# The split weights start 44 instead of 48 bytes behind a multiple of 64, and the table of constants lies behind them

## What is computed

```python
for li in range(2):                                   # the first block
    x = x + 0.5 * swiglu(rmsnorm(x, g[0]), ffn_w_in[li, 0], ffn_w_out[li, 0])     # 1024 -> 2*2816 -> 1024
    x = x + (hgrn2_mixer if li == 0 else mla_mixer)(rmsnorm(x, g[1]), ...)
    x = x + 0.5 * swiglu(rmsnorm(x, g[2]), ffn_w_in[li, 1], ffn_w_out[li, 1])
    x = x + sigmoid(rmsnorm(x, g[3]) @ ple_w_gate[li]) * (p[li] @ ple_w_in[li])
x = rmsnorm(x, final_norm)
for layer in range(2):                                # the second block
    x = x + (even_mixer if layer == 0 else odd_mixer)(rms_norm(x, ...), ...)
    x = x + conv_ffn(rms_norm(x, ffn_norm[layer]), w_up, conv_w, conv_b, w_down)  # 1024 -> 2*2816 -> 1024
```

## The kernel before

| tile | offset modulo 64 | what uses it |
|---|---|---|
| raw, x, x_hi, x_lo, h_hi, h_lo, h_val, c_hi, c_lo, q_both, x_lo_2 | 0 | loads, activations |
| cst | 12 | first constant `mean1024` at 12, `freq` is one column, all others behind it at 16 |
| rstd, rstd_tok | 16 | norms |
| sumsq, ln_ms, ln_tok | 32 | norms |
| w_hi, w_lo, all slots and 128-column tiles | 48 | the split weights |
| tmp, zero, eps | 48 | squares, clearing |
| work, small, k_rope, cos, sin | 52 | everything inside the mixers and hidden layers |

## Time and profile before

### The profile page before, as it was taken

One profiled execution on the slowest core, in us unless ns is written; L12 is line 12 of the kernel. 1 busy time (PEld: TensorE's weight loads), 2 busy tenths in 40 slices (PEclk: granted clock), 3 DMA queues, 4 the chain that ended last, 5 costly groups with the idle time before them and its releaser, 6 DMA issues.

```text
span 1822.1 us, 36683 instructions
## 1 busy us (share of the span) xinstructions
PE 1750.2 (96%) x14492; PEld 1714.1 (94%) x14492; DVE 1190.6 (65%) x1764; ACT 957.6 (53%) x1097; POOL 351.6 (19%) x280
## 2 busy tenths in 40 slices
PE   7999899989999899999999999999899999989998
PEld 7999899979999899998998999988799999989998
DVE  6665688976565666556456555665477766567776
ACT  5444667764444754444345444565455455655553
POOL 2000500020004600036663000566400020020001
PEclk9999999999999999999999999999999999999999
DMA  5656323335555445544444555434245443345552
GB/s 218 225 190 242 128 101 115 99 119 208 198 190 185 156 176 193 188 141 135 137 138 154 187 187 185 170 128 151 93 170 199 177 180 139 117 162 185 185 206 92
DMA packets 45168, 298.25 MB, mean 164 GB/s; under 512 B 5024, under 2 KB 5408, under 8 KB 15920
## 3 DMA queue, kind: packets, MB, share of 16 engines
q1 hardware_dynamic: 45104, 297.38, 46.1%
HBM read 296.31 MB, written 1.05 MB: 163 GB/s over the span
## 4 chain that ended last, share of the span: by engine, by line
PE 80%; DVE 10%; ACT 5%; issue 3%; DMA 1%; POOL 0%; SPq 0%; ACTq 0%; DVEq 0%
PE wk L379 15%; PE wk L380 15%; PE wk L381 15%; PE acc L379 8%; PE acc L380 8%; PE acc L381 8%; DVE sumsq L678 2%; DVE x_lo L457 1%; PE wk L1033 1%; PE wk L391 1%; PE wk L390 1%; PE wk L389 1%; DVE x L422 1%; ACT w_hi L325 1%; ACT tmp L619 1%
## 5 line engine op out<-in xcount | busy, mean ns | idle before, releaser
L325 ACT ACTIVATE w_hi<-raw 128x2048 fp32r<-128x2048 f32 (+5 forms) x300 | 533.3, 1788 | 405.8 <-PE wk L381 333.8
L380 PE MATMUL wk<-x_lo,w_hi 128*128 128x256 f32 x2560 | 715.9, 280 | 0.0
L379 PE MATMUL wk<-x_hi,w_hi 128*128 128x256 f32 x2208 | 624.7, 283 | 19.0 <-DVE x_lo L457 13.3
L2603 POOL TENSOR_TENSOR w_lo<-raw,w_hi 128x512 fp32r<-128x512 f32 (+1 forms) x274 | 350.8, 1316 | 1455.7 <-ACT w_hi L325 1455.7
L381 PE MATMUL wk<-x_hi,w_lo 128*128 128x256 f32 x2208 | 618.0, 280 | 0.0
L351 DVE TENSOR_TENSOR w_lo<-raw,w_hi 128x2048 fp32r<-128x2048 f32 (+2 forms) x218 | 483.9, 2221 | 171.5 <-ACT w_hi L325 171.5
L380 PEld LDWEIGHTS wk<-x_lo,w_hi 128*128 128x128 f32 x2560 | 483.5, 189 | 0.4
L379 PEld LDWEIGHTS wk<-x_hi,w_hi 128*128 128x128 f32 x2208 | 421.4, 191 | 25.2 <-DVE x_lo L457 15.4
L381 PEld LDWEIGHTS wk<-x_hi,w_lo 128*128 128x128 f32 x2208 | 416.8, 189 | 0.0
L379 PE MATMUL acc<-h_hi,w_hi 128*128 128x256 f32 x1376 | 389.5, 283 | 16.3 <-DVE h_lo L2192 4.8
L381 PE MATMUL acc<-h_hi,w_lo 128*128 128x256 f32 x1376 | 385.9, 280 | 0.0
(11 more groups left out here) (323 smaller groups left out, 2138.4 us busy)
## 6 DMA issues: line engine op xcount, KB each, us to landing
raw<-w_ffn_loop SPq DMA_DIRECT2D x120, 1024.0 KB, 4.8
raw<-w_conv_loop SPq DMA_DIRECT2D x60, 1024.0 KB, 4.8
raw<-w_mla_loop SPq DMA_DIRECT2D x18, 768.0 KB, 4.3
raw<-w_hgrn_loop SPq DMA_DIRECT2D x10, 896.0 KB, 4.6
raw<-w_ple_gate SPq DMA_DIRECT2D x8, 1024.0 KB, 4.7
raw<-w_odd_loop SPq DMA_DIRECT2D x10, 768.0 KB, 4.2
raw<-w_even_loop SPq DMA_DIRECT2D x6, 1024.0 KB, 4.8
raw<-w_odd_proj SPq DMA_DIRECT2D x6, 1024.0 KB, 4.8
```

Of the source, the lines that this page charges most:

```text
L325: nc.scalar.activation(w_hi[slot][:, 0:n], raw[slot][:, 0:n], ACT.Copy).then_inc(S("hi_ready"), 1)
L379: nc.tensor.matmul(dst, hi, a_hi, start=start, stop=False, skip_group_check=True)
L380: nc.tensor.matmul(dst, hi, a_lo, start=False, stop=False, skip_group_check=True)
L2603: last = nc.gpsimd.tensor_tensor(w_lo[slot][:, a:b], raw[slot][:, a:b], w_hi[slot][:, a:b].bitcast(F32), ALU.subtract)
```

## The change

The line that allocates `cst` moves from behind `par` to behind `w_lo`. Nothing else is edited; every engine's list of instructions is the same, in the same order, with the same waits. What differs is addresses:

```diff
         par = sb("par", [P, N_PARAMS])
-        cst = sb("cst", [P, N_CONSTS])
         rstd = sb("rstd", [P, SEQ])
         rstd_tok = sb("rstd_tok", [P, 2 * TB])
         sumsq = sb("sumsq", [P, SEQ])
         ln_ms = sb("ln_ms", [P, SEQ])
         ln_tok = sb("ln_tok", [P, 2 * TB])
         w_hi = [sb(f"w_hi{s}", [P, SLOT_TILES * P], F32R) for s in range(SLOTS)]
         w_lo = [sb(f"w_lo{s}", [P, SLOT_TILES * P], F32R) for s in range(SLOTS)]
+        cst = sb("cst", [P, N_CONSTS])
         tmp = sb("tmp", [P, 8, SEQ])
```

## The result

The changed kernel takes 1848.93 us (median of 4 runs, 1847.19 to 1851.08), beside 1822.47 us for the kernel before (4 runs, 1817.01 to 1828.51): 1.0133 times the time, 95% interval 1.0091 to 1.0176. That is slower by 1.3%, outside the range of the prediction (1790 to 1840 us; its likeliest case alone 1806 to 1834).

A forecast was written before the change was run, and what follows sets the result against it. PE's chain of matmuls was taken to bound the kernel; all terms were priced 0, so 1822.1 + 0 + 1.9 = 1824 us, set at 1820 us nearer the runs' median of 1819.7, range 1790 to 1840 us.

The forecast's parts named there:

- likeliest case: Whole kernel: no rule of PE's paces changes, about as many loops at either pace; 1806 to 1834 us, chance 0.53.
- What bounds the kernel, and the two paces: PE's matmul chain takes the whole time; the six feed-forward loops run at 113.1 or 117.6 ns a matmul.
- Item 1: PE's weight operands, about 13,000 matmuls: an offset off a multiple of 16 costs 0, between -10 and +10 us.
- the sign that I had set: In the six loops, a third pace would show item 1 wrong and the shift to have its own price.
- Item 2: PE's choice between two paces, perhaps set by weight offset against activations: bounded by -29 and +29 us, taken as 0.
- Items 3, 4 and 5: ACT and DVE on weights and norms, POOL writing w_lo, table and small tiles: 0 each; +3 us for POOL in the range.
- B: Rival: at 44 PE can't reach the fast pace, all loops slow; +29 us, 1849 us; chance 0.21, in full or good part.
- A: Rival: the new offset keeps PE off the slow pace; -29 us, 1791 us; chance 0.26, in full or good part.
- The rule on 16-byte lines: Weight row at 44 touches 33 lines instead of 32; one column's time per extra line gives +5 us, 1825 us.

The follow-up runs named there:

- e15: Kernel before with one unused column ahead of x_lo and 63 behind it, so x_lo alone stands 4 bytes up modulo 256; 1831.71 us, ratio 1.0062.
- e18: Changed kernel with all activations moved 4 bytes down modulo 256 by unused columns, so the distance is 240 again; 1812.37 us, ratio 0.9985.
- e3: Kernel before with 4 unused columns ahead of w_hi and 12 behind w_lo: weights at 0 modulo 64; 1849.91 us, ratio 1.0170.
- e4: Kernel before with 12 unused columns ahead of w_hi and 4 behind w_lo: weights at 32 modulo 64; 1851.66 us, ratio 1.0169.
- e5: Kernel before with 8 unused columns ahead of w_hi and 8 behind w_lo: weights at 16 modulo 64; 1847.00 us, ratio 1.0111.
- e14: Kernel before with rstd_tok and ln_tok allocated behind w_lo: weights down by 32 bytes, distance 208; 1864.62 us, ratio 1.0246.
- e13: Kernel before with the table between w_hi and w_lo and one unused column ahead of w_hi: w_hi at 48, w_lo at 52; 1850.94 us, ratio 1.0182.
- e16: Kernel before with one unused column ahead of h_lo and 63 behind it, so only h_lo is 4 bytes off; 1840.28 us, ratio 1.0133.

## Why the prediction was wrong

- **What bounds the kernel, and the two paces.** Right. PE's step from matmul to matmul in the feed-forward loops is what moved, and 23.8 us worked out from the counts is close to the span's 23.3. Two details were off: 13,536 matmuls touch a weight tile, not some 13,000, and a pace doesn't change only where PE starts again after a wait. In the kernel before it goes from 113 to 118 ns at 845.9 us with no break, where `token_tile` matmuls give way to `channel_tile` ones, and e15 changes it, with no break either, between the halves of nearly every turn of five loops.
- **Item 1, an operand off a multiple of 16 costs nothing in isolation.** The number stood (189 ns a load, and e18, with all operands of these matmuls 4 bytes below the offsets modulo 16 of the kernel before, loses nothing), but it answered the wrong question. I asked for the weights' offset modulo 16. The matmuls of 128 columns with a weight moving do not show the effect at any distance: by the records they follow each other at a mean of 111.6 to 111.8 ns in every run. The plain float32 ones have both operands in `work`, whose place no experiment changed against itself. So their equal pace said nothing on matmuls of 256 columns. By the sign that I had set, a third value of the pace would mean that the shift has a price of its own; the third value came, and e18 shows that this reading of it is wrong.
- **Item 2, the two paces, taken as 0.** This is the step that failed. I named the right mechanism ("if the offset of the weights against that of the activations sets which pace PE falls into") and its price, +29 us, and then gave it 0, with the argument that both paces exist at 48 and so the offset doesn't decide alone. The runs have +23.8 us in the loops in place of the 0. Both paces being there says that the offset doesn't force the fast pace; it doesn't say that the fast pace exists at other offsets. Ten distances other than 240 were tried: at nine of them no profiled loop has the fast pace, and at 112 it is rarer.
- **Items 3, 4 and 5.** Right: POOL 1333 ns for 1334, ACT 418, DVE 418 for 416 in the row compared, and PE's idle time went down, not up.
- **The rivals.** B came about: 1849 us was its number and 1848.9 is the median. That they meet so closely is in part luck: B was +29 us on a base of 1820, and the runs are +26.5 us on a median of 1822.5 (the profiled executions +23.3). Its size was about right for a partly different reason: not the slow one of the two paces but a third, uneven one, half a nanosecond slower, and with it the loops that were slow already lose a little too. In B the loops had 19 of the 29 us and the mixers and edges 10. The runs have 23.8 us in the loops; outside them PE's busy time grew by some 4 us (28.0 - 23.8), and 4.7 us less idle time paid that back. A did not happen with any distance: no profiled execution has all six loops fast.
- **The rule on 16-byte lines.** What it would make of the change was +5 us for a line more, 1825 us. The runs speak against it as the cause: e3, e4 and e5, whose weights have the same offset modulo 16 as in the kernel before, lose as much, e18, where all operands of these matmuls have the other one, loses nothing, and the load stays at 189 ns. The Trainium skill, page "SBUF — State Buffer", in the paragraph on cachelines under "Door 1: The DMA port swizzle", has a penalty for each crossing to a new 16-byte line. No run here shows such a penalty for a row that starts off a line, and here the measurement decides.
- **The range.** It left the full B out so as not to be wider than 8 in 10. With a mechanism that acts on all loops at once there was no reason to expect half of B; to hold B at all, the upper end belonged above 1849.

## What to carry to other kernels

When matmuls run back to back, look at the steps between their starts, not at their durations: a histogram of them shows paces, and two paces for the same work mean that something besides the work sets them. An allocation is then part of the tuning: the distance between the stationary and the moving tile modulo 256 bytes was worth 1.1 to 2.5% here (e5, 1.0111, to e14, 1.0246), so before a table or a small tile is moved, work out what it does to that distance, and pin it with padding of its own instead of leaving it to the sum of the lengths ahead.

## What the runs showed of the hardware

- Loads of a 128x128 stationary tile and matmuls of 256 moving columns of float32r, in turn, have more than one lasting pace at the 2.4 GHz level, by counts: 113.1 and 117.6 ns (even), 117.1 to 118.7 (uneven, mostly 115 to 123 ns), 119.7 (150 us / 1253, e14, even). A pace can last over more than a thousand matmuls. In the profiles it changes at breaks (26.77 and 642.50 us of the kernel before) and where the operands of the matmuls change (845.9 us there, and between the halves of a turn in e15); a break doesn't always change it.
- Which of them occurs in the six loops hangs on the distance of the two operands' addresses modulo 256: at 240 113.1 and 117.6; at 112 the same two, the slow one more often; at 0, 16, 32, 44, 48, 208, 224, 236 and 244 only the uneven or slower ones. 4 bytes either way from 240 lose the fast pace.
- Matmuls of 128 moving columns do not show it: 111.6 to 111.8 ns in every run (those with a weight moving, by the records).
- One operand that is off, in one of the three matmuls of a tile, is enough (w_lo in e13, x_lo in e15), and the uneven pace can be carried into matmuls whose own operands fit (e16).
- What lies behind it is open. Reads of the two operands that meet in the same part of the memory would fit a rule on distances with a period, but no run here shows the memory itself.
